# A hand-ordered recurrence on five queues: one segment of RWKV-7 and mLSTM work put into another order

## The chip, the cores and the metric

One core of one Trainium2 chip. The metric is the device time of one execution of the whole layer, in microseconds (us), taken as the median of several executions of one compiled kernel. The engines are TensorE (PE), VectorE (DVE), ScalarE (ACT), GpSimd (POOL) and the sync engine (SP), whose queue issues loads.

## What is computed

The layer has four stages in a row: a SwiGLU feed-forward, a token mixer, cross-attention over 256 memory tokens, and a second feed-forward. The change is in the token mixer, whose core is two recurrences over 1024 tokens. Cut to what matters:

```python
# RWKV-7, 8 heads of 64
state = state * w_t + (state @ -kk_t)[..., None] * (kk_t * a_t) + v_t[..., None] * k_t
y_t = state @ r_t                       # then a per-head norm, a bonus term and a gate
# mLSTM, 4 heads of 128
c = dec * c + sc * (w_end * v) @ k.T
num = p @ v + w_inter * (c_prev @ q)    # p = exp(log_d - m) * (q @ k.T)
h = num / max(|den|, exp(-m))           # then a per-head norm and a gate
```

## The kernel before, in words

The 1024 tokens are cut into eight segments of 128. One iteration of a hand-written software pipeline does the front of segment i (`front`) and the back of segment i-1 (`back`). Every engine has its own function `iteration`, and its instructions run in the order in which they are written there; between engines there are only semaphores. A list of names per engine (`F_PE`, `M_DVE` and so on) turns a name into the count that a waiting engine waits for.

The delta rule inside a segment needs the inverse of a triangular 128x128 matrix per head. It is built by doubling, in levels n = 1 to 6, with the heads in two sets, a and b. At each level TensorE forms W (from `AL` or `Ar`, and `Ur`) and V (a transpose of `Ur`) of each set, all L862; ScalarE copies them into `Wr` and `Tr`; TensorE forms E from `Tr` and `Wr`; and VectorE updates `Ur` with E (`update`, L1779 or L1783). GpSimd makes the masked matrices `AL` (L573, two for each of the levels 1 to 4). Between the two E products of a level TensorE does one step of the mLSTM (`mlstm(n)`): num at 1, dC at 3, key norms and a transpose `yT` at 4, two grams at 5 and 6. Calls of `stay_awake` are products whose result nobody reads (L786).

After level 6 come F (L774), V (L928), B (L768), and UQ (L774), which ends in `Uf` on VectorE. Then TensorE does the low-rank products `lora` of the next segment (L747, L749), Wst (L941), Z (L945) and the gate products (L949). With that the next iteration begins: Zm with Uf (L794), W1m with S0s (L797), the state products, the bonus product (L824), and transposes named kT, vT, aT, vT, bT, kT. bT (beta) writes the bank that held the bonus, so it waits for `bv` on VectorE. Then come the mean, the gram A, the variance product (L849), S, and the level 0 products A0.

On VectorE one period runs: `Uf`, two operations of the key norm (`rinv`, `kk`, by `key_root(i, 2)`), `dec` to `cc`, `gsig`, `ga`, `gu`, `kmod`, `kka` (in tile `nw`), `alpha`, `beta`, two operations on `St`, `bv`, then `Ys`, the masks of A, the variance, `U0`, `Pb`, `qe`, and the levels. The output norm of the segment before (four operations of 0.7 us, `output_norm`) stands behind level 4. GpSimd waits for its result, and finishes the output (`output`, L535 to L539), then does `bvb` (L542) and `ab` (L545) of the next iteration, and behind `kmod` four operations L547 to L553 (`rkb` twice, `kap`, `rho`).

SP loads `zs` (896 KB) for the next segment once the mask `Ab` of this one is made, then the rows `ab` and `tk`, then `zm`.

## Time and profile before

| what | us |
|---|---|
| median of 3 runs (2991.62 to 3000.18) | 2999.92 |
| profiled execution, its own time | 2997.45 |
| its span, first to last instruction | 2995.5 |
| from the start of the first segment's `Uf` to that of the eighth (seven periods) | 405.9 |

The span and the execution's own time differ by 1.95 us. The recurrence lies at about 1310 to 1827 us of the span; what is before and after it is not touched by the change. A period is counted from the start of one `Uf` to the start of the next.

### The profile page before, as it was taken

To read this page: it belongs to the slowest core of one execution; us is meant where nothing else is said; L and a number is where in the kernel's file an instruction comes from. 1 tells how busy PE (TensorE), PEld (TensorE's weight loads), DVE (VectorE), ACT (ScalarE), POOL (GpSimd) and SP (SyncE) were. 2 spreads that over 40 slices of the span, in tenths; PEclk is the share of its full clock that TensorE was granted. 3 is DMA by queue.
4 is the path that set the end of the run, shared out by engine and by line. 5 is a ranking of instruction groups with operands and counts; after the bars stand their busy time and mean duration, and the time that the engine had idled before them with its cause. 6 is when DMAs were issued, how large, how long until landed. Compare 5 with 4: busy or idle time off the path is not lost.

```text
span 2995.5 us, 38320 instructions
## 1 busy us (share of the span) xinstructions
PE 2876.2 (96%) x14927; PEld 2414.7 (81%) x14927; DVE 1281.2 (43%) x1206; ACT 579.5 (19%) x906; POOL 1219.8 (41%) x651
## 2 busy tenths in 40 slices
PE   7999999999999999969999999999999999999996
PEld 6888888888888888858888887887888888888885
DVE  5431331235556522036777765541454321431334
ACT  3100000002001121125555541110411100000011
POOL 3443333334444366624445544333044433334432
PEclk9999999999999999979989999999999999999998
DMA  3111111113222233322111203321011111111111
GB/s 133 45 46 49 49 49 49 49 44 110 99 98 98 98 110 131 118 86 45 48 33 49 51 3 131 134 77 42 0 49 44 47 49 49 49 49 49 50 40 72
DMA packets 99115, 196.61 MB, mean 66 GB/s; under 512 B 14288, under 2 KB 56400, under 8 KB 98792
## 3 DMA queue, kind: packets, MB, share of 16 engines
q1 hardware_dynamic: 80912, 139.05, 15.6%
q10 hardware_dynamic: 18136, 56.60, 5.0%
q8 instruction: 49, 0.80, 0.1%
q14 instruction: 18, 0.15, 0.0%
HBM read 160.93 MB, written 34.67 MB: 65 GB/s over the span
## 4 chain that ended last, share of the span: by engine, by line
PE 42%; issue 7%; POOL 4%; DVE 2%; ACT 1%; DMA 0%; POOLq 0%; DVEq 0%; SPq 0%; ACTq 0%
PE G L636 12%; PE G L638 12%; PE G L637 12%; PE G L1029 1%; POOL AL L573 1%; PE G L862 1%; PE G L1052 1%; POOL rkb L547 0%; PE G L849 0%; DVE xT L1986 0%; POOL ysq L558 0%; POOL rho L553 0%; POOL Ys L537 0%; PE G L1041 0%; POOL ab L545 0%
## 5 line engine op out<-in xcount | busy, mean ns | idle before, releaser
L594 POOL TENSOR_TENSOR whi<-raw,zero 128x1024 fp32r<-128x1024 f32 (+1 forms) x213 | 398.5, 1871 | 1410.3 <-PE G L638 1406.8
L636 PE MATMUL G<-hhi,whi 128*128 128x512 f32 x2288 | 893.6, 391 | 17.3 <-DVE hlo L1506 17.3
L638 PE MATMUL G<-hhi,wlo 128*128 128x512 f32 x2288 | 891.2, 390 | 0.0
L637 PE MATMUL G<-hlo,whi 128*128 128x512 f32 x2288 | 891.2, 389 | 0.0
L597 POOL TENSOR_TENSOR wlo<-raw,whi 128x1024 fp32r<-128x1024 f32 (+1 forms) x213 | 517.1, 2428 | 16.7
L636 PEld LDWEIGHTS G<-hhi,whi 128*128 128x128 f32 x2288 | 430.2, 188 | 108.8 <-issue 15.3
L638 PEld LDWEIGHTS G<-hhi,wlo 128*128 128x128 f32 x2288 | 430.1, 188 | 89.7
L637 PEld LDWEIGHTS G<-hlo,whi 128*128 128x128 f32 x2288 | 430.2, 188 | 89.3 <-issue 0.7
L636 PE MATMUL G<-ahi,whi 128*128 128x512 f32 x960 | 374.5, 390 | 2.7 <-DVEq L425 2.7
L638 PE MATMUL G<-ahi,wlo 128*128 128x512 f32 x960 | 374.2, 390 | 0.0
L637 PE MATMUL G<-alo,whi 128*128 128x512 f32 x960 | 374.2, 390 | 0.0
L636 PEld LDWEIGHTS G<-ahi,whi 128*128 128x128 f32 x960 | 180.6, 188 | 40.7 <-issue 3.1
L637 PEld LDWEIGHTS G<-alo,whi 128*128 128x128 f32 x960 | 180.5, 188 | 37.7 <-issue 0.2
L638 PEld LDWEIGHTS G<-ahi,wlo 128*128 128x128 f32 x960 | 180.6, 188 | 37.5
L1156 ACT ACTIVATE s<-s 128x1024 f32<-128x1024 f32 x44 | 46.7, 1061 | 759.7 <-DVE s L1580 759.7
L1537 DVE SCALAR_TENSOR_TENSOR xT<-G,xT 128x1024 f32 x32 | 39.2, 1225 | 292.2 <-PE G L638 292.2
L1580 DVE TENSOR_TENSOR s<-G,nrx 128x1024 f32<-128x1024 f32 x44 | 53.9, 1225 | 245.8 <-PE G L638 244.9
L1582 DVE TENSOR_TENSOR s<-s,nrx 128x1024 f32<-128x1024 f32 x44 | 132.6, 3014 | 49.6 <-ACT s L1156 49.6
L1588 DVE TENSOR_TENSOR alo<-s,ahi 128x1024 f32 x44 | 127.3, 2894 | 60.2 <-ACT ahi L1158 60.2
L1586 DVE TENSOR_TENSOR s<-s,G 128x1024 f32<-128x1024 f32 x44 | 53.8, 1222 | 224.1 <-PE G L638 223.9
L1158 ACT ACTIVATE ahi<-s 128x1024 f32 x44 | 46.7, 1062 | 418.4 <-DVE s L1586 418.4
L1597 DVE TENSOR_TENSOR po<-G,nrm 128x1024 f32<-128x1024 f32 x24 | 29.4, 1224 | 219.9 <-PE G L638 217.6
(325 smaller groups left out, 3229.7 us busy)
## 6 DMA issues: line engine op xcount, KB each, us to landing
raw<-in_wg SPq DMA_DIRECT2D x44, 512.0 KB, 3.5
raw<-in_wu SPq DMA_DIRECT2D x44, 512.0 KB, 3.5
raw<-in_wd SPq DMA_DIRECT2D x32, 512.0 KB, 3.5
raw<-in_ml_in SPq DMA_DIRECT2D x16, 512.0 KB, 3.5
zml_d<-po ACTq DMA_DIRECT2D x16, 512.0 KB, 2.6
gates_d<-po ACTq DMA_DIRECT2D x16, 512.0 KB, 2.7
zm<-zml_d SPq DMA_DIRECT2D x8, 1024.0 KB, 5.4
sg<-gates_d ACTq DMA_DIRECT2D x16, 512.0 KB, 5.0
```

The lines of the kernel that those rows point to most:

```text
L594: nc.gpsimd.tensor_tensor(hi, raw[:, k, 0:w], zero[:].to_broadcast([P, w]), ALU.add).then_inc(hi_made, 1)
L597: nc.gpsimd.tensor_tensor(lo, raw[:, k, 0:w], hi.bitcast(F32), ALU.subtract).then_inc(split_made, 1)
L636: nc.tensor.matmul(dst, wh, hi, start=start, stop=False)
L637: nc.tensor.matmul(dst, wh, lo, start=False, stop=False)
L638: return nc.tensor.matmul(dst, wl, hi, start=False, stop=stop)
L1156: activation(s0[:], s0[:], ACT.Silu).then_inc(f_silu, 1)
L1158: activation(ahi[:, i * 2 + r, :], s1[:], ACT.Copy).then_inc(a_hi, 1)
L1537: stt(x_, flat(bank_dve(c.dve + r)[:]), scale, x_, ALU.mult, ALU.add).then_inc(dve_free, 1)
L1580: tt(s0[:], flat(bank_act(c.act + r)[:]), nrx[:], ALU.mult).then_inc(act_free, 1)
L1582: tt(s0[:], s0[:], nrx[:], ALU.mult).then_inc(f_scaled, 1)
L1586: tt(s1[:], s0[:], flat(bank_dve(c.dve + r)[:]), ALU.mult).then_inc(dve_free, 1)
L1588: tt(alo[:, i * 2 + r, :], s1[:], ahi[:, i * 2 + r, :].bitcast(F32), ALU.subtract).then_inc(a_lo, 1)
```

## The change

The order of the segment's work is changed on every queue; sizes and arithmetic stay.

- VectorE: level 0 updates (`first`) ahead of the variance; `qe` right behind `bv`; the denominator and `hm` behind level 1 where they stood behind level 2; the statistics split around the second update of level 2, followed by the sum C; the four operations of the output norm set singly, at levels 3, 5, 6 and 6; `pend` ahead of the wait for A; `S0s` ahead of the wait for B and `key_root(i+1, 1)` behind it; `key_root(i, 2)` behind `kmod` of the next iteration.
- TensorE: S ahead of the variance product; W1m with S0s ahead of Zm with Uf; gate products ahead of Wst; dC at level 2, key norms at level 3; F in two halves with a wait each; the fillers ahead of A0 and at level 2 are gone in iterations with `back`, and there is one at level 4.
- ScalarE: table load and the two small activations into `lora` ahead of the copy into `Tr`; the output root behind level 1's copies; the gate's copy ahead of `Zm`'s.
- GpSimd: the masks `AL` of level 1 first, then `kw`; `ahead` (kk, ksq) behind level 2, `dec` behind level 3, `zg` last.
- SP: `zs` waits for `bv` and `vtok` in place of `Ab`.
- The last segment: three fillers at level 3 where the key norms are missing, and a small memset where the key root is.

The name lists are reordered to match and left out here; unchanged lines are cut.

```diff
...
@@ -460,7 +460,8 @@
             if front:
-                sp.wait_ge(*f_dve.at("Ab", i - 1))
+                sp.wait_ge(*f_dve.at("bv", i - 1))
+                sp.wait_ge(*f_act.at("vtok", i - 1))
...
@@ -559,10 +560,6 @@
                 return
-            pool.wait_ge(*m_act.at("D", i))
-            tt(kw[:], mktok[:], Db[:, :, SEG - 1:SEG].to_broadcast([P, MH, SEG]), ALU.mult).then_inc(*M.sig("kw"))
-            pool.wait_ge(zm_in, i * 16 + 16)
-            tt(zm[:, 12:16, :], zm[:, 12:16, :], vbc("ml_norm", SEG), ALU.mult).then_inc(*M.sig("zg"))
...
@@ -572,10 +569,17 @@
                        ALU.mult).then_inc(*F.sig(f"am{n}{x}"))
-            pool.wait_ge(*m_pe.at("num", i))
-            tt(CN[:], CN[:], Eb[:, :, SEG - 1:SEG].to_broadcast([P, MH, SEG + 1]), ALU.mult).then_inc(*M.sig("dec"))
-            if more:
-                ahead(i + 1)
+                if n == 1:
+                    pool.wait_ge(*m_act.at("D", i))
+                    tt(kw[:], mktok[:], Db[:, :, SEG - 1:SEG].to_broadcast([P, MH, SEG]), ALU.mult).then_inc(*M.sig("kw"))
+                if n == 2 and more:
+                    ahead(i + 1)
+                if n == 3:
+                    pool.wait_ge(*m_pe.at("num", i))
+                    tt(CN[:], CN[:], Eb[:, :, SEG - 1:SEG].to_broadcast([P, MH, SEG + 1]),
+                       ALU.mult).then_inc(*M.sig("dec"))
+            pool.wait_ge(zm_in, i * 16 + 16)
+            tt(zm[:, 12:16, :], zm[:, 12:16, :], vbc("ml_norm", SEG), ALU.mult).then_inc(*M.sig("zg"))
...
@@ -789,13 +793,14 @@
             if back:
+                pe.wait_ge(*f_act.at("W1c", j))
+                for n, e, r, rows in heads:
+                    nc.tensor.matmul(G[3][:, e, r * HD:(r + 1) * HD], W1m[rows, r, :], S0s[rows, r, :],
+                                     start=r == 0, stop=False, skip_group_check=True)
...
                 for n, e, r, rows in heads:
-                    nc.tensor.matmul(G[3][:, e, r * HD:(r + 1) * HD], Uf[:, n, :], Zm[:, n, :], start=r == 0, stop=False,
-                                     skip_group_check=True)
-                for n, e, r, rows in heads:
-                    last = nc.tensor.matmul(G[3][:, e, r * HD:(r + 1) * HD], W1m[rows, r, :], S0s[rows, r, :],
-                                            start=False, stop=r == RC - 1, skip_group_check=True)
+                    last = nc.tensor.matmul(G[3][:, e, r * HD:(r + 1) * HD], Uf[:, n, :], Zm[:, n, :], start=False,
+                                            stop=r == RC - 1, skip_group_check=True)
...
@@ -844,15 +849,17 @@
                 gram(alpha, beta, g1).then_inc(*F.sig("A"))
+            if front:
+                pe.wait_ge(*m_act.at("ktok", i))
+                for h in range(MH):
+                    last = nc.tensor.matmul(m0[:, h * SEG:(h + 1) * SEG], zm[:, MH + h, :], zm[:, h, :], start=True,
+                                            stop=True)
+                last.then_inc(*M.sig("S"))
...
                 return
-            pe.wait_ge(*m_act.at("ktok", i))
-            for h in range(MH):
-                last = nc.tensor.matmul(m0[:, h * SEG:(h + 1) * SEG], zm[:, MH + h, :], zm[:, h, :], start=True, stop=True)
-            last.then_inc(*M.sig("S"))
...
@@ -863,7 +870,8 @@
-            stay_awake(g2[:, 0, :], 3)
+            if not back:
+                stay_awake(g2[:, 0, :], 3)
...
@@ -872,25 +880,27 @@
                     pe.wait_ge(*m_act.at("vtok", i))
-                    pe.wait_ge(*m_dve.at("qe", i))
+                    pe.wait_ge(*m_dve.at("P", i))
...
                     last.then_inc(*M.sig("num"))
-                elif n == 3:
+                elif n == 2:
...
                     last.then_inc(*M.sig("dC"))
-                elif n == 4:
+                elif n == 3:
...
                         key_norms(i + 1)
+                    else:
+                        stay_awake(g0[:, 1, :], 3)
+                elif n == 4:
+                    stay_awake(g0[:, 1, :], 1 if back else 3)
...
                     turn(m0, hm).then_inc(*M.sig("yT"))
-                    if not back:
-                        stay_awake(g0[:, 1, :], 2)
...
@@ -900,8 +910,6 @@
                     gram(kap, rho, G[3]).then_inc(*F.sig("Mv"))
-                else:
-                    stay_awake(g0[:, 1, :], 3 if back else 4)
...
@@ -911,7 +919,7 @@
                     four(g1, e, AL[:, n % 2] if n <= MASKED else Ar, lambda n: Ur[:, n, :]).then_inc(*F.sig(f"W{n}{x}"))
-                    if n == 1:
+                    if n == 1 and e == 1:
...
@@ -921,9 +929,10 @@
                 four(g0, 1, Tr, lambda n: Wr[:, n, :]).then_inc(*F.sig(f"E{n}b"))
-            for x in SETS:
+            for e, x in enumerate(SETS):
...
-            eight(g1, Am, Ur[:].bitcast(F32)).then_inc(*F.sig("F"))
+                last = four(g1, e, Am, lambda n: Ur[:, n, :].bitcast(F32))
+            last.then_inc(*F.sig("F"))
...
@@ -936,6 +945,10 @@
                 ahead(i + 1)
+            for r in range(RC):
+                last = nc.tensor.matmul(g2[:, 0, r * P:(r + 1) * P], loraw[:, 1, r * P:(r + 1) * P], gsig[:],
+                                        start=True, stop=True)
+            last.then_inc(*F.sig("gate"))
...
@@ -945,10 +958,6 @@
             last.then_inc(*F.sig("Z"))
-            for r in range(RC):
-                last = nc.tensor.matmul(g2[:, 0, r * P:(r + 1) * P], loraw[:, 1, r * P:(r + 1) * P], gsig[:],
-                                        start=True, stop=True)
-            last.then_inc(*F.sig("gate"))
...
@@ -1245,17 +1254,20 @@
+        def lora_in(i):
+            act.wait_ge(zs_in, i * 16 + 16)
+            activation(lora[0:HD, :], zs[0:HD, 12, :], ACT.Tanh).then_inc(*l_act.sig("th"))
+            activation(lora[HD:P, :], zs[HD:P, 12, :], ACT.Copy).then_inc(*l_act.sig("ad"))
...
             tanh_exp_tables()
+            lora_in(i)
...
-            act.wait_ge(zs_in, i * 16 + 16)
-            activation(lora[0:HD, :], zs[0:HD, 12, :], ACT.Tanh).then_inc(*l_act.sig("th"))
-            activation(lora[HD:P, :], zs[HD:P, 12, :], ACT.Copy).then_inc(*l_act.sig("ad"))
...
@@ -1329,8 +1341,6 @@
                 activation(half(Ar, e), half(Am, e), ACT.Copy).then_inc(*F.sig(f"Ar{x}"))
-            if back:
-                output_root()
...
@@ -1338,6 +1348,8 @@
                 if n == 1:
+                    if back:
+                        output_root()
...
@@ -1348,19 +1360,20 @@
                     key_roots(i + 1)
+            if more:
+                tanh_exp_tables()
+                lora_in(i + 1)
...
             if more:
-                tanh_exp_tables()
...
             activation(flat(W1m[:]), g2[:, 1, :], ACT.Copy).then_inc(*F.sig("W1c"))
-            act.wait_ge(*f_pe.at("Z", i))
-            activation(flat(Zm[:]), g0[:, 0, :], ACT.Copy).then_inc(*F.sig("Zc"))
-            act.wait_ge(*f_pe.at("gate", i))
...
             activation(flat(gout[:]), g2[:, 0, :], ACT.Copy).then_inc(*F.sig("gev"))
+            act.wait_ge(*f_pe.at("Z", i))
+            activation(flat(Zm[:]), g0[:, 0, :], ACT.Copy).then_inc(*F.sig("Zc"))
...
@@ -1708,10 +1721,20 @@
-            def output_norm():
-                dve.wait_ge(*b_act.at("rsv", j))
-                newton(B, ("g1", "g2", "g3"), yrs, yve, ynw, j)
-                tt(Ys[:], Ys[:], yrs[:], ALU.mult).then_inc(*B.sig("y1"))
+            def output_norm(k):
+                r, w, v = flat(yrs[:]), flat(ynw[:]), flat(yve[:])
+                if k == 0:
+                    dve.wait_ge(*b_act.at("rsv", j))
+                    stt(w, r, -0.5, r, ALU.mult, ALU.mult).then_inc(*B.sig("g1"))
+                elif k == 1:
+                    dve.wait_ge(*B.at("g1", j))
+                    tt(w, w, v, ALU.mult).then_inc(*B.sig("g2"))
+                elif k == 2:
+                    dve.wait_ge(*B.at("g2", j))
+                    stt(r, w, 1.5, r, ALU.add, ALU.mult).then_inc(*B.sig("g3"))
+                else:
+                    dve.wait_ge(*B.at("g3", j))
+                    tt(flat(Ys[:]), flat(Ys[:]), r, ALU.mult).then_inc(*B.sig("y1"))
...
@@ -1734,6 +1757,8 @@
                     ALU.mult).then_inc(*F.sig("kmod"))
+                if back:
+                    key_root(i, 2)
...
@@ -1752,16 +1777,21 @@
                 tt(bv[:], three(g0[:, 1, :]), zs[:, 8:12, :], ALU.mult).then_inc(*F.sig("bv"))
+                dve.wait_ge(*m_act.at("E", i))
+                dve.wait_ge(zm_in, i * 16 + 16)
+                stt(flat(qe[:]), zm[:, 0:MH, :].rearrange("p h t -> p (h t)"), ML_SCALE, flat(Eb[:]), ALU.mult,
+                    ALU.mult).then_inc(*M.sig("qe"))
...
                 output_variance()
-                output_norm()
+                for k in range(4):
+                    output_norm(k)
...
-            dve.wait_ge(*f_pe.at("A", i))
...
                ALU.mult).then_inc(*F.sig("pend"))
+            dve.wait_ge(*f_pe.at("A", i))
...
@@ -1788,19 +1818,28 @@
                                           three(g1[:, e, :])).then_inc(*F.sig(f"A{x}"))
+            first(0)
+            first(1)
...
                 output_variance()
-            first(0)
-            first(1)
...
             stt(flat(Pb[:]), m0, ML_SCALE, flat(Db[:]), ALU.mult, ALU.mult).then_inc(*M.sig("P"))
-            stt(flat(qe[:]), zm[:, 0:MH, :].rearrange("p h t -> p (h t)"), ML_SCALE, flat(Eb[:]), ALU.mult,
-                ALU.mult).then_inc(*M.sig("qe"))
...
+                if n == 6 and back:
+                    output_norm(2)
...
+                if n == 2:
+                    for h in range(2):
+                        nc.vector.bn_stats(mst[:, h, :], hm[:, h, :])
+                if n == 3 and back:
+                    output_norm(0)
+                if n == 5 and back:
+                    output_norm(1)
+                if n == 6 and back:
+                    output_norm(3)
...
-                if n == 2:
+                if n == 1:
...
@@ -1810,9 +1849,14 @@
                     dve.wait_ge(*M.at("hm", i))
-                    for h in range(MH):
+                if n == 2:
+                    for h in range(2, MH):
...
                     last.then_inc(*M.sig("st"))
+                    dve.wait_ge(*m_pool.at("dec", i))
+                    dve.wait_ge(*m_pe.at("dC", i))
+                    CN4 = CN[:].rearrange("p (b h) v -> p b h v", b=2)
+                    tt(CN4, CN4, pairs_of(G[3]), ALU.add).then_inc(*M.sig("C"))
...
@@ -1821,10 +1865,6 @@
                 if n == 3:
-                    dve.wait_ge(*m_pool.at("dec", i))
-                    dve.wait_ge(*m_pe.at("dC", i))
-                    CN4 = CN[:].rearrange("p (b h) v -> p b h v", b=2)
-                    tt(CN4, CN4, pairs_of(G[3]), ALU.add).then_inc(*M.sig("C"))
...
@@ -1841,8 +1881,6 @@
                     tt(yres[:, 0:RC, bass.ds(i * SEG, SEG)], three(m0), zm[:, 12:16, :], ALU.mult).then_inc(*M.sig("y1"))
-                    if back:
-                        output_norm()
...
@@ -1851,16 +1889,16 @@
             tt(Qr[:], copies(C_ID), three(flat(g1[:])), ALU.subtract).then_inc(*F.sig("Q"))
+            dve.wait_ge(*b_dve.at("S", j))
+            tt(S0s[:], St[:], Pi[:, :, 0:1].to_broadcast([P, RC, HD]), ALU.mult).then_inc(*F.sig("S0s"))
+            dve.wait_ge(*f_pe.at("B", i))
...
                 key_root(i + 1, 1)
-            dve.wait_ge(*b_dve.at("S", j))
-            dve.wait_ge(*f_pe.at("B", i))
-            tt(S0s[:], St[:], Pi[:, :, 0:1].to_broadcast([P, RC, HD]), ALU.mult).then_inc(*F.sig("S0s"))
+            else:
+                nc.vector.memset(mnw[:], 0.0)
...
             tt(flat(Uf[:]), flat(Ur[:]).bitcast(F32), flat(g0[:]), ALU.add).then_inc(*F.sig("Uf"))
-            if more:
-                key_root(i + 1, 2)
...
```

## Rows read from the trace of the kernel before

**Rows 1.** The page: busy time by engine.

```profile
PE 2876.2 (96%) x14927; PEld 2414.7 (81%) x14927; DVE 1281.2 (43%) x1206; ACT 579.5 (19%) x906; POOL 1219.8 (41%) x651
```

**Rows 2.** Windows: seven periods, then three single ones; after POOL: clock, DMA share, GB/s.

```profile
1382.50:1788.40 405.90, 376.19 (x3428) 337.71 (x3428) 295.23 (x529) 226.80 (x464) 199.01 (x160) 0.94 0.16 37
1559.50:1620.40 60.90, 56.88 (x490) 51.11 (x490) 42.44 (x77) 32.65 (x66) 28.31 (x23) 0.89 0.15 41
1620.40:1675.70 55.30, 50.95 (x490) 45.52 (x490) 42.41 (x77) 32.84 (x68) 28.28 (x23) 1.00 0.16 45
1675.70:1734.00 58.30, 53.83 (x490) 48.25 (x490) 42.50 (x78) 32.92 (x69) 28.26 (x23) 0.94 0.23 43
```

**Rows 3.** Windows: behind the wait ahead of level 6, and low-clock stretches.

```profile
1604.50:1607.30 2.80, 1.64 (x15) 1.58 (x15) 2.71 (x6) 0.88 (x2) 1.97 (x2) 1.00 1.00 301
1607.30:1617.60 10.30, 9.79 (x52) 9.24 (x51) 4.35 (x7) 1.29 (x3) 3.88 (x4) 0.50 0.00 0
...
1723.40:1730.20 6.80, 6.29 (x37) 5.88 (x37) 2.55 (x4) 0.17 (x1) 3.05 (x3) 0.50 0.00 0
```

**Rows 4.** Timeline of TensorE: start, length, line, tile, count, [idle before, releaser].

```profile
1670.16 2.05 PE L774 MATMUL G<-Ur,Am 128*128 128x128 f32 x16 [0.51 <-DVE Ur L1783]
...
1676.13 0.37 PE L747 MATMUL G<-lora,loraw 64*128 64x128 f32 x1 [0.77 <-ACT lora L1258]
...
1677.22 1.09 PE L941 MATMUL G<-Uf,atok 128*64 128x128 f32 x16
...
1690.60 0.60 PE L762 MATMUL G<-cst,beta 128*128 128x128 f32 x4
...
1694.40 1.12 PE L849 MATMUL G<-ysq,cst 128*128 128x512 f32 x2 [0.73 <-POOL ysq L558]
...
1696.17 0.94 PE L786 MATMUL G<-idr 128*128 128x512 f32 x3
...
1698.36 0.66 PE L862 MATMUL G<-Ur,AL 128*128 128x128 f32 x4 [0.41 <-DVE Ur L1772]
...
1701.04 0.49 PE L877 MATMUL G<-mvx,Pb 128*128 128x129 f32 x2 [0.18 <-DVE qe L1798]
...
1711.32 0.66 PE L862 MATMUL G<-Ur,AL 128*128 128x128 f32 x4 [0.54 <-DVE Ur L1779]
...
1720.80 0.66 PE L862 MATMUL G<-Ur,Ar 128*128 128x128 f32 x4 [1.16 <-DVE Ur L1783]
```

**Rows 5.** Timeline of TensorE, end of the last segment, where no next segment is prepared.

```profile
1789.66 1.09 PE L941 MATMUL G<-Uf,atok 128*64 128x128 f32 x16 [1.78 <-DVE Uf L1861]
```

**Rows 6.** Timeline of VectorE in the period of rows 4.

```profile
1674.54 1.29 DVE L1705 COPY_PREDICATED Bm<-cst,G 128x1024 f32<-128x1024 uint32 x1
1675.73 1.20 DVE L1861 TENSOR_TENSOR Uf<-Ur,G 128x1024 f32<-128x1024 f32 x1
...
1683.45 0.69 DVE L1735 SCALAR_TENSOR_TENSOR kmod<-rkb,zs 128x512 f32<-128x512 f32 x1
...
1684.67 1.76 DVE L1740 TENSOR_TENSOR alpha<-kk,Pp 128x512 f32<-128x512 f32 x1
1686.35 1.52 DVE L1742 TENSOR_TENSOR beta<-nw,Pi 128x512 f32<-128x512 f32 x1
...
1689.15 0.69 DVE L1754 TENSOR_TENSOR bv<-G,zs 128x512 f32<-128x512 f32 x1
...
1693.72 0.65 DVE L1763 TENSOR_TENSOR pend<-Pp,cst 128x4 f32<-128x4 f32 x1 [0.49 <-PE G L768]
...
1699.35 1.63 DVE L1798 SCALAR_TENSOR_TENSOR qe<-zm,Eb 128x512 f32<-128x512 f32 x1
```

**Rows 7.** Timeline of GpSimd over the same period.

```profile
1668.86 1.04 POOL L542 TENSOR_TENSOR bvb<-bv,vec 128x512 f32<-128x512 f32 x1
...
1684.22 1.65 POOL L547 TENSOR_TENSOR rkb<-zs,kmod 128x512 f32<-128x512 f32 x1 [13.09 <-DVE kmod L1735]
```

**Rows 8.** Timeline of ScalarE over the same period.

```profile
1680.28 0.60 ACT L1359 ACTIVATE Zm<-G 128x512 f32<-128x512 f32 x1 [0.28 <-PE G L945]
```

More of the change, by code:

```diff
@@ L106 @@
            + [f"E{n}b"]]
-        + ["F", "V", "B", "UQ", "Wst", "Z", "gate"])
+        + ["F", "V", "B", "UQ", "gate", "Wst", "Z"])
 F_ACT = (["P", "Pi", "atok", "vtok", "btok", "ktok"] + [f"Ar{x}" for x in SETS]
-         + [f"{y}{n}{x}" for n in range(1, LEVELS) for x in SETS for y in ("Wc", "Tc")] + ["Tc", "W1c", "Zc", "gev"])
+         + [f"{y}{n}{x}" for n in range(1, LEVELS) for x in SETS for y in ("Wc", "Tc")] + ["Tc", "W1c", "gev", "Zc"])
 F_DVE = (["dec", "scan", "hend", "cc", "gs", "av", "gu", "kmod", "kka",
@@ L119 @@
 M_ACT = ["E", "nm", "ktok", "vtok", "D", "aden", "lnv", "rsv"]
-M_DVE = ["P", "qe", "dmax", "rec", "hm", "st", "mv", "ve", "C", "g1", "g2", "g3", "yn", "y1"]
-M_POOL = ["arg", "kw", "zg", "dec"]
+M_DVE = ["qe", "P", "dmax", "rec", "hm", "st", "C", "mv", "ve", "g1", "g2", "g3", "yn", "y1"]
+M_POOL = ["arg", "kw", "dec", "zg"]
 XQ_ACT = ["q"]
```

## The prediction, as put on record

> **What bounds the kernel now.** I read the page first: TensorE is busy for 96% of the span [rows 1], so nothing outside the recurrence can be won by order, and inside it only what makes TensorE wait, work for nothing, or run at a low clock. Second, the windows by period. Seven periods take 405.9 us at a mean granted clock of 0.94. A period at full clock takes 55.3; two with low stretches take 58.3 and 60.9 with the same number of products [rows 2]. At 55.3 the seven would take 387.1, so the clock costs 18.8 us. The windows inside two of them show what stands ahead of a fall: 1.64 us of busy time in 2.8, then half clock (1.2 of 2.4 GHz) for 10.3 us; elsewhere 6.8 us [rows 3]. Both begin just behind the longest wait of the period, 1.16 us at the entry of level 6, where TensorE waits for `Ur` while VectorE is in the four operations of the output norm. A period at full clock has that wait too, so the wait alone doesn't decide.
>
> Third, TensorE's timeline. I count t from the first product of Wst (L941, 1677.22). Its waits in a full-clock period are 0.77 for `lora`, 0.73 for `ysq`, 0.41 for `Ur` ahead of level 1, 0.18 for `qe`, 0.54 at level 4, 1.16 at level 6, and 0.51 ahead of F [rows 4]: 4.3 us. Three fillers ahead of A0 take 0.78 until the next product starts at 1696.95, and three more at level 2 some 0.75.
>
> Fourth, VectorE's and GpSimd's timelines side by side behind `kmod`. `kmod` takes 0.69 and, like every operation of that shape left alone, ends in time. `alpha` takes 1.76 and `beta` 1.52 for the same 128x512 elements [rows 6], and GpSimd's first `rkb` takes 1.65 where its like take 1.04 [rows 7]. The starts and ends interlock: `nw` ends at 1684.75, `rkb` at 1685.87 (1.1 later), `alpha` at 1686.43 (0.56 later), the next `rkb` at 1687.33, `beta` at 1687.87. `qe`, between two masks of GpSimd, takes 1.63, and `pend` of four columns 0.65 [rows 6]. So a VectorE operation with two operands in SBUF and a GpSimd operation run in turn, 0.55 us and about 1.05 us each; those with a PSUM operand (`bv`, `Uf`, `Bm`) don't wait.
>
> **The change part by part**, for one period at full clock, as the place where each product starts.
>
> *Around Wst.* `lora` no longer waits (0.77), and the gate products (1.02 to 0.94 us, start to start) fill the time in which `Uf` is made. From Wst to the first state product the gate is gone: -0.94. W1m's products cover the copy of `Zm`, which starts at t = 3.06 [rows 8]. The table load and both small activations lie in ScalarE's idle time behind level 6 and cost nothing; without that cover they would cost the 0.77 again. `zs` is loaded some five microseconds earlier, ahead of `ab` in the same queue, and `ab` is ready when it was.
>
> *Up to bT.* `gsig` waits for its tanh, which stands behind the copy of `Zm`: 3.06 + 0.50 + 0.33 = 3.89. `kmod` starts 1.32 later at 5.21 (before: 6.23 [rows 4, 6]) and ends at 5.9. Then `key_root(i, 2)` puts two operations with two SBUF operands here that ran beside an idle GpSimd before. Five such VectorE operations (`rinv`, `kk`, `kka`, `alpha`, `beta`) and four of GpSimd in turn: 5 x 0.55 + 4 x 1.05 = 6.95, so `beta` ends at 12.85, against 10.65 before. `St` twice and `bv` are behind it in the queue (1.97 from `beta`'s end to `bv`'s before, of which about 0.5 was waiting for products and port [rows 6]): `bv` ends near 14.3, and bT starts at 14.4. TensorE without this wait would be there at 12.44; before it was there at 13.38 [rows 4]. So the 0.94 is lost and 1.02 more: +1.96, and a new wait of 1.8 us. Queued behind bT are kT, the mean, A; all wait with it.
>
> *bT to W1.* S hides the wait of 0.73, three fillers go (0.78), `pend` leaves the path (0.57), and `U0` no longer stands behind the variance (0.6, partly beside other work): from bT to W1 6.3 us in place of 7.76 (1690.60 to 1698.36 [rows 4]): -1.46. The masks first on GpSimd are what makes the 6.3 possible: `am1a` ends near 20.1, W1 starts at 20.7.
>
> *Level 1.* num no longer waits for `qe`, and less stands between: -0.33.
>
> *Levels 2 to 4.* dC (0.87) replaces three fillers (0.75), and the wait of 0.54 goes. Put back: `aden`'s first operation comes when GpSimd has `kk` and `ksq` in hand (up to 1.05), which makes dC wait about 0.5; the norm's first operation waits for a mask (0.5) and with it W4b 0.2; `yT` waits 0.4; one filler 0.25. Sum +0.17.
>
> *Levels 5 and 6.* The norm in pieces frees `Ur` at once: -1.16 and some slack, together -1.35. F in halves starts without its 0.51: -0.69.
>
> *Up to the next Wst.* `Ys` is normalised at F - 0.3, 5 us later than now. So GpSimd's output chain (`bvb` starts 3.84 behind its first operation) reaches into VectorE's operations: `S0s` waits 0.1, and `key_root(i+1, 1)`, now ahead of `Bm`, finds `bvb` in hand and waits 1.05. `Bm` (0.34 behind `S0s` now) starts 1.2 to 1.9 later, and `Uf` with it; Wst starts 1.49 behind `Uf` [rows 4, 6]. From F to Wst: 8.5 in place of 7.06 (1670.16 to 1677.22 [rows 4]): +1.45, with TensorE idle for about 1.3 us ahead of Wst. Without the turn-taking it would be +0.6.
>
> Sum: -0.94 + 1.96 - 1.46 - 0.33 + 0.17 - 1.35 - 0.69 + 1.45 = **-1.2**, and I take -1.1, so -7.7 for seven periods. Bounds: with no turn-taking at all bT costs nothing and Wst 0.6: -4.0 a period (-28). With every pairing against VectorE once more (`rec`, `yn` behind `zg`: 1.05), 0.
>
> *Ends.* In the last segment the gate fills 0.94 of the 1.78 us ahead of Wst [rows 5]; in the first one, without fillers gone or a norm, `pend`, F and num give about 1.3, an estimate from the terms above. Together -2.3.
>
> A rule of the Trainium skill speaks against the change. The page "SBUF — State Buffer", section "Who interferes with whom", says that a VectorE operation with two SBUF inputs contends with a GpSimd one that reads SBUF, which the trace shows as above; it adds that `tensor_scalar` in its fast mode takes the same port. No row shows that here, since GpSimd is idle at `yn`. By it `yn`, four such operations now close to `zg`, could wait up to 1.05 more, and seven periods would lose 7 us of the gain.
>
> *The clock.* This is the largest unknown. The waits of 1.16 and 0.51, ahead of every fall I see, go. Two new ones come, 1.8 us ahead of bT and 1.3 ahead of Wst. One low stretch of 6.8 us costs 58.3 - 55.3 = 3.0 us [rows 2, 3]. From below: none, -18.8. From above: two in each period, 14 x 3.0 = 42.0, which is +23.2. The rows nearest are the waits of 0.73, 0.77 and 1.16: the first two no fall, the third most times. The bT wait is longer than any of them but stands among dense 512-column and transpose work, so I take one stretch in six of seven periods: 18.0, or -0.8.
>
> Total: -7.7 - 2.3 - 0.8 = -10.8, against the profiled execution's own 2997.45: **2986 us** (that execution lies 2.5 below the median shown, well inside what three runs spread).
>
> **The rivals.**
> 1. *The low clock goes.* Order gains as above and no new wait pulls the clock down: 2997.45 - 7.7 - 2.3 - 18.8 = 2969. For it: the falls all begin behind one wait, and that one is removed. Against: the new ones are as long. If in addition the turn-taking bites less, 2948 at the least.
> 2. *Slower: the clock falls twice a period.* The waits ahead of bT and of Wst each bring 6.8 us at half clock: -10.0 + 23.2 = +13, 3010. It decides as soon as more than nine stretches (28.8 / 3.0) of that length come in seven periods. For it: fillers that kept TensorE at work are gone, and 1.3 and 1.8 are above 1.16. Against: the period from 1620.4 to 1675.7, in which the wait of 1.16 brought no fall.
> 3. *It doesn't do what it says.* The waits only move, VectorE and GpSimd in turn eat all: 0 a period, 2995 to 3001.
>
> **How the numbers follow.** Forecast 0.42 (alone: 2974 to 2997), rival 1 0.24, rival 2 0.16, rival 3 0.18. The range from 2958 to 3010 leaves out about two in ten, half of it below rival 1 and half above rival 2. About 0.3% (9 us) is what a measurement of this kernel can tell from no change. Faster: two thirds of the forecast, rival 1 and a little of rival 3, 0.54. Slower: most of rival 2, 0.15. Within: 0.31.
>
> **What would show each step.** `lora`'s products start with no wait; a wait of 1 us or more stands ahead of L762 bT, released by `bv`, with `rinv`, `kk`, `alpha` and `beta` stretched to about 1.6 each. L862 behind level 5 starts with no wait. `key_root`'s L1680 takes 1.6 and a wait stands ahead of L941. GpSimd's masks start ahead of `kw`. A full-clock period reads 54 us. Wrong would be: no stretched operations (then 51 to 52), or a granted clock in the recurrence of 1.0 (rival 1) or below 0.92 (rival 2).

## The result, and the profile after

The changed kernel takes 2949.66 us (median of 4 runs, 2946.59 to 2951.97) against 2998.95 (4 runs, 2991.62 to 3000.18): ratio 0.984, interval 0.9821 to 0.9859. The prediction's sign was right, but the gain is 49 us where it gave 11, and 2949.66 lies below the range of 2958 to 3010. The profiled execution took 2946.59, its span 2944.8: 50.7 less than the span before.

The page, busy time by engine, in the form of [rows 1]:

```profile
PE 2843.2 (97%) x14892; PEld 2380.9 (81%) x14892; DVE 1292.1 (44%) x1207; ACT 579.1 (20%) x906; POOL 1227.4 (42%) x651
```

Windows of the changed kernel, with the columns of [rows 2]: the seven periods, two single ones, and a low stretch in the last segment.

```profile
1377.20:1746.10 368.90, 351.55 (x3399) 312.35 (x3400) 305.08 (x531) 226.65 (x464) 201.95 (x158) 1.00 0.19 41
1589.30:1642.10 52.80, 50.31 (x488) 44.58 (x487) 43.93 (x77) 32.87 (x68) 29.38 (x24) 1.00 0.27 47
1642.10:1694.90 52.80, 50.29 (x487) 44.54 (x486) 43.91 (x77) 32.83 (x68) 29.37 (x24) 1.00 0.22 47
1760.90:1767.70 6.80, 6.10 (x12) 4.16 (x13) 2.56 (x4) 1.26 (x2) 0.64 (x1) 0.50 0.20 62
```

In a window row the busy times stand in the order PE, PEld, DVE, ACT, POOL. The clock column reads 1.00 over all seven periods, where [rows 2] has 0.94. The seven take 368.9 in place of 405.9, so 37.0 less. Of that 18.8 is the low clock, as it was worked out ahead, and 18.2 is order: 387.1 less 368.9, about 2.5 for each period (55.3 to 52.8). The last of the seven is shorter than the others in both kernels (54.45 before, 51.14 after, each at full clock), so the split between clock and order is good to about 1 us. The rest of the 50.7 lies outside: 5.3 ahead of the first `Uf` (1382.5 to 1377.2) and 8.4 behind the last.

TensorE's timeline of one period, to be laid beside [rows 4] (start, length, line, tile, count, [idle before, releaser]):

```profile
1641.55 1.16 PE L949 MATMUL G<-gsig,loraw 128*128 128x128 f32 x8
1643.36 1.09 PE L954 MATMUL G<-Uf,atok 128*64 128x128 f32 x16 [0.66 <-DVE Uf L1901]
...
1655.12 0.60 PE L766 MATMUL G<-cst,alpha 128*128 128x128 f32 x4
1656.64 0.65 PE L766 MATMUL G<-cst,zs 128*128 128x128 f32 x4 [0.93 <-DVE St L1773]
1657.62 0.66 PE L766 MATMUL G<-cst,beta 128*128 128x128 f32 x4 [0.33 <-DVE bv L1779]
...
1663.32 0.66 PE L869 MATMUL G<-idr,AL 128*128 128x128 f32 x4 [0.30 <-DVE Am L1819]
1663.96 0.66 PE L869 MATMUL G<-Ur,AL 128*128 128x128 f32 x4
...
1684.24 0.61 PE L869 MATMUL G<-Ur,Ar 128*128 128x128 f32 x4
...
1688.21 2.00 PE L869 MATMUL G<-Ur,Am 128*128 128x128 f32 x16
...
1692.24 1.10 PE L778 MATMUL G<-Qr,Tr 128*128 128x128 f32 x8
1693.28 0.37 PE L751 MATMUL G<-lora,loraw 64*128 64x128 f32 x1
```

The waits of 1.16 ahead of level 6, 0.51 ahead of F, 0.77 ahead of `lora` and 0.73 ahead of the variance are gone. There are two large new ones: 0.66 ahead of Wst, and 0.93 + 0.33 between aT and bT. A small one of 0.30 ahead of the level 0 products stands where the three fillers stood. Read by starts, the wait between aT and bT costs more than its idle time: vT starts 1.52 behind aT and bT 0.98 behind vT, where transposes that follow without a wait start 0.44 apart (1658.12 to 1658.56), so 1.62 in all.

VectorE and then GpSimd between `kmod` and `bv`, beside [rows 6, 7]:

```profile
1648.57 0.69 DVE L1758 SCALAR_TENSOR_TENSOR kmod<-rkb,zs 128x512 f32<-128x512 f32 x1
1649.18 0.69 DVE L1696 SCALAR_TENSOR_TENSOR rinv<-nw,rinv 128x512 f32<-128x512 f32 x1
1649.90 1.65 DVE L1698 TENSOR_TENSOR kk<-kk,rinv 128x512 f32<-128x512 f32 x1
1651.58 1.42 DVE L1763 TENSOR_TENSOR nw<-kk,ga 128x512 f32<-128x512 f32 x1
1652.92 1.67 DVE L1765 TENSOR_TENSOR alpha<-kk,Pp 128x512 f32<-128x512 f32 x1
1654.51 1.67 DVE L1767 TENSOR_TENSOR beta<-nw,Pi 128x512 f32<-128x512 f32 x1
...
1656.89 0.68 DVE L1779 TENSOR_TENSOR bv<-G,zs 128x512 f32<-128x512 f32 x1
```

```profile
1649.34 1.65 POOL L548 TENSOR_TENSOR rkb<-zs,kmod 128x512 f32<-128x512 f32 x1 [7.22 <-DVE kmod L1758]
1651.08 1.37 POOL L550 TENSOR_TENSOR rkb<-rkb,vec 128x512 f32<-128x512 f32 x1
1652.41 1.63 POOL L552 TENSOR_TENSOR kap<-kmod,Pi 128x512 f32<-128x512 f32 x1
1654.00 1.63 POOL L554 TENSOR_TENSOR rho<-zs,Pp 128x512 f32<-128x512 f32 x1
```

The turn-taking is there as foretold. The operations on either engine are stretched alike and their ends interlock, and `beta` ends at 1656.18, 12.82 behind the first Wst product (foretold 12.85).

### The profile page after: what moved, and what is told of

The parts are those of the page before. It is cut to its first block, busy times and chain, and to the rows that moved or that the text cites. A ratio compares the mean times of both kernels' runs of the same rounds, so it can differ in the third digit from the quotient of the medians.

```text
span 2944.8 us, 38257 instructions
## 1 busy us (share of the span) xinstructions
PE 2843.2 (97%) x14892; PEld 2380.9 (81%) x14892; DVE 1292.1 (44%) x1207; ACT 579.1 (20%) x906; POOL 1227.4 (42%) x651
## 4 chain that ended last, share of the span: by engine, by line
PE 47%; DVE 5%; issue 2%; ACT 1%; POOL 1%; DMA 0%; DVEq 0%; SPq 0%; ACTq 0%; POOLq 0%
PE G L640 12%; PE G L642 12%; PE G L641 12%; PE G L869 4%; PE G L1038 1%; PE G L772 1%; PE G L1061 1%; PE G L958 1%; PE G L766 1%; DVE kk L1698 0%; DVE ylo L1931 0%; DVE beta L1767 0%; DVE Am L1819 0%; PE G L892 0%; PE G L954 0%
```

## The experiments

Each ran on a chip with its own runs of the kernel before, and a ratio holds inside its batch. A period and its low clock are read from each profile as above.

**a1: the output norm back in one block.** In the changed kernel all four operations stand behind level 4's `yres` again.

```diff
-                if n == 6 and back:
-                    output_norm(2)
...
                     tt(yres[:, 0:RC, bass.ds(i * SEG, SEG)], three(m0), zm[:, 12:16, :], ALU.mult).then_inc(*M.sig("y1"))
+                    if back:
+                        for k in range(4):
+                            output_norm(k)
```

> The changed kernel with the four operations of the output norm back in one block behind level 4. Theory A (the clock fell because TensorE stood still at the entry of level 6, and it no longer does): the wait there is back at about 1.3 us, a full-clock period is 53.4 to 54.0 in place of 52.8, and low-clock stretches of 6.8 us return in about half or more of the seven periods, 3 us each: 2962 to 2975. Theory B (the clock came back by the rest of the order, or by the length of the period): the wait is back, the seven periods stay at a granted clock of 1.0, and only the wait is paid: 2953 to 2958.

Measured: 2976.2 (9 runs, 2962.1 to 2984.63), ratio 0.9915 (0.9889 to 0.9941). TensorE's wait ahead of level 6, then the windows of the low stretch behind it and of the one period that had the wait but no fall:

```profile
1593.72 0.66 PE L869 MATMUL G<-Ur,Ar 128*128 128x128 f32 x4 [1.16 <-DVE Ur L1813]
```

```profile
1594.30:1604.50 10.20, 10.20 (x56) 9.86 (x55) 4.04 (x6) 4.29 (x7) 4.79 (x4) 0.50 0.09 26
1608.40:1661.60 53.20, 50.24 (x489) 44.71 (x488) 42.97 (x78) 32.78 (x67) 28.08 (x23) 1.00 0.27 47
```

The old wait comes back to the hundredth in six periods, and in five of them the clock falls within 2.1 us behind it, some 44 us at 0.50 in all. The seventh period has no such wait, but a stretch of 30.7 us at 0.50 that begins 0.2 us behind a wait of 0.60 ahead of dC (1747.63). The changed kernel has that wait too (0.59 at 1724.52) and no fall behind it, so those 30.7 us can't be put down to the norm. The profiled execution is the slowest of the nine. At full clock the edit costs only 0.4 a period, 53.2 against 52.8, since the wait of 0.66 ahead of Wst goes as the 1.16 comes (Wst starts at 1609.73 without one). So nearly all of the loss (26 us between the medians, 22 by the two ratios) is clock.

**a2: `bv` later by 1.5 us.** Three memsets of 128x512 stand ahead of it in the changed kernel.

```diff
                 dve.wait_ge(*b_pool.at("bvb", j))
+                if back:
+                    for t in (ynw, yve, yrs):
+                        nc.vector.memset(t[:], 0.0)
                 tt(bv[:]...
```

> The changed kernel with three memsets of 128x512 on VectorE ahead of bv (work added, result unchanged), so that TensorE's wait ahead of the transpose bT grows from about 1.3 us to about 2.8. If only the length of a wait decided over the clock, every period would fall to half clock behind it: 1.5 a period plus 3 a period, 2980 or more. If what decides is the wait together with the products around it, the clock stays at 1.0 in the seven periods and the time is 2950 + 7 x 1.5 = 2960.

Measured: 2971.01 (5 runs, 2967.51 to 2977.21), ratio 0.9911 (0.9884 to 0.9939). The waits in front of vT and bT, and the low stretch that begins inside the second:

```profile
1616.44 0.65 PE L766 MATMUL G<-cst,zs 128*128 128x128 f32 x4 [0.93 <-DVE St L1773]
1618.99 1.12 PE L766 MATMUL G<-cst,beta 128*128 128x128 f32 x4 [1.90 <-DVE bv L1782]
```

```profile
1618.00:1624.80 6.80, 5.81 (x27) 4.09 (x28) 2.37 (x6) 4.39 (x9) 1.04 (x1) 0.50 0.48 135
```

Every period now has a low stretch (30.6 us in seven). In six of them one begins within 1.1 us of the end of the wait ahead of bT, in the seventh 8.5 us behind it. The wait at this place does reach the clock once it is 2.8 us long; at 1.26 it doesn't. The 1.8 of the prediction lies between and was not run.

**b1: before, with only the norm in pieces.**

```diff
+                if n == 6 and back:
+                    output_norm(2)
                 update(n, 0)
+                if n == 3 and back:
+                    output_norm(0)
+                if n == 5 and back:
+                    output_norm(1)
+                if n == 6 and back:
+                    output_norm(3)
                 update(n, 1)
```

> The kernel before with this one part of the change: the four operations of the output norm set singly at levels 3, 5, 6 and 6. Theory A: the wait of 1.16 us at level 6 is gone, a full-clock period is about 54.2 in place of 55.3 (less where the output chain of GpSimd now meets VectorE at the end), and the seven periods run at a clock of 1.0: 2999 - 8 - 19 = 2972, and no less than 15 us gained. Theory B: the clock stays at 0.94, and only the wait is gained: 2991.

Measured: 3025.68 (6 runs, 3013.6 to 3030.56), ratio 1.0088 (1.0063 to 1.0114): slower. VectorE with one GpSimd row, then TensorE, ahead of Wst:

```profile
1555.01 1.47 DVE L1680 TENSOR_TENSOR nw<-nw,ssc 128x512 f32<-128x512 f32 x1
1556.40 1.49 DVE L1875 TENSOR_TENSOR S0s<-St,Pi 128x256 f32<-128x256 f32 x1
1555.89 1.72 POOL L545 TENSOR_TENSOR ab<-ab,cst 128x512 f32<-128x512 f32 x1
1557.82 1.29 DVE L1705 COPY_PREDICATED Bm<-cst,G 128x1024 f32<-128x1024 uint32 x1
1559.00 1.21 DVE L1878 TENSOR_TENSOR Uf<-Ur,G 128x1024 f32<-128x1024 f32 x1
```

```profile
1551.78 2.05 PE L774 MATMUL G<-Ur,Am 128*128 128x128 f32 x16 [0.51 <-DVE Ur L1794]
1557.74 0.37 PE L747 MATMUL G<-lora,loraw 64*128 64x128 f32 x1 [0.77 <-ACT lora L1258]
1560.26 1.97 PE L941 MATMUL G<-Uf,atok 128*64 128x128 f32 x16 [1.36 <-DVE Uf L1878]
```

The level-6 wait is gone, but GpSimd finishes the output later and now takes turns with `nw` and `S0s`. There are three waits in 9 us, the last of them 1.34 to 1.36. Six periods have it, and in four of them the clock falls at it, for 17.1 us each. Three stretches of 3.4 us begin elsewhere, 78.6 us in seven periods. A full-clock period reads 55.7.

**b2: before, with five fillers in level 5.** Nothing else moves.

```diff
                     gram(beta, rho, G[3]).then_inc(*F.sig("Mu"))
+                    if back:
+                        stay_awake(g0[:, 1, :], 5)
```

> The kernel before with five products that nobody reads (1.1 us at full clock) between the gram and the second E product of level 5, where TensorE would otherwise stand still at the entry of level 6. No engine's other order is changed. If standing still brings the clock down: clock 1.0 in the seven periods, a period of 55.3 to 55.6, 2975 to 2982. If it doesn't: 2999 to 3003 with clock 0.94. This separates the price of the clock from that of the wait.

Measured: 2981.03 (7 runs, 2979.15 to 2983.36), ratio 0.9945 (0.9928 to 0.9962). TensorE's timeline and the windows:

```profile
1537.40 1.45 PE L786 MATMUL G<-idr 128*128 128x512 f32 x5
```

```profile
1383.70:1773.70 390.00, 367.09 (x3463) 328.19 (x3463) 295.27 (x530) 226.56 (x464) 198.92 (x160) 0.99 0.18 39
1494.20:1549.50 55.30, 52.10 (x495) 46.45 (x495) 42.41 (x78) 32.84 (x67) 28.26 (x23) 1.00 0.17 45
```

The wait of 1.16 is gone, the fillers take its time (the period stays 55.3), and low clock shrinks from 47.7 to 6.8 us. This prices the clock without any change of order: 405.9 to 390.0 in the periods.

**a5: gate products behind Z again**, in the changed kernel, with their copy behind `Zm`'s.

```diff
-            for r in range(RC):
-                last = nc.tensor.matmul(g2[:, 0, ...], loraw[:, 1, ...], gsig[:], start=True, stop=True)
-            last.then_inc(*F.sig("gate"))
             pe.wait_ge(*f_dve.at("Uf", i))
```

> The changed kernel with the gate products, and their copy, back behind Z. The wait ahead of Wst grows from 0.66 to about 1.6 us. Theory A (a wait of over about a microsecond among the small products of the levels and the state brings the clock down): low-clock stretches begin behind Wst in most periods; 2970 to 2990. Theory B (only the wait at level 6 does so): order alone, 0.2 to 0.9 a period, 2951 to 2956.

Measured: 2981.05 (10 runs, 2972.77 to 2987.45), ratio 0.9926 (0.9906 to 0.9946). TensorE's timeline, and two periods in windows:

```profile
1605.19 1.93 PE L950 MATMUL G<-Uf,atok 128*64 128x128 f32 x16 [1.72 <-DVE Uf L1902]
```

```profile
1490.10:1550.10 60.00, 57.64 (x485) 52.26 (x485) 43.30 (x78) 32.87 (x68) 28.51 (x23) 0.86 0.17 42
1550.10:1603.90 53.80, 50.18 (x485) 44.50 (x485) 43.90 (x77) 32.94 (x68) 29.36 (x24) 1.00 0.22 46
```

Losing the cover costs 1.0 a period at full clock. The wait of 1.72 to 1.75 stands in six of the seven periods; in four of them the clock falls within 1.8 us behind it (58.2 us, and 3.4 more that begin elsewhere).

**a6: the stretch from A to level 1 as before** (variance ahead of S and of `U0`, `pend` behind the wait for A, three fillers, `first(0)` and `first(1)` behind the variance, and the wait for `ve` ahead of V of both sets), in the changed kernel.

```diff
+            if back:
+                pe.wait_ge(*b_pool.at("ysq", j))
+                nc.tensor.matmul(g2[:, 1, :], ...).then_inc(*B.sig("var"))
             if front:
                 pe.wait_ge(*m_act.at("ktok", i))
...
-            if back:
-                pe.wait_ge(*b_pool.at("ysq", j))
-                nc.tensor.matmul(g2[:, 1, :], ...).then_inc(*B.sig("var"))
...
-            if not back:
-                stay_awake(g2[:, 0, :], 3)
+            stay_awake(g2[:, 0, :], 3)
...
-                    if n == 1 and e == 1:
+                    if n == 1:
```

> The changed kernel with the stretch from A to level 1 as before: S behind the variance product, three fillers ahead of A0, the level 0 updates behind the variance, pend behind the wait for A. If this stretch is worth what its term said, a full-clock period is 54.2 to 54.3 in place of 52.8 (1.42 us, from the transpose bT to W1) and the time 2960 with the clock at 1.0. If the stretch only moves the wait (GpSimd's masks, made first, would have to wait for it anyway), less than 0.7 a period, 2950 to 2955. The rival on the clock: with waits of 0.73 and 0.41 back here, low-clock stretches return, 2965 or more.

Measured: 2966.47 (4 runs, 2965.99 to 2966.99), ratio 0.9882 (0.9844 to 0.9919). Windows of a full-clock period and of the only low stretch in the seven:

```profile
1486.10:1540.40 54.30, 50.65 (x490) 45.10 (x489) 44.35 (x77) 33.10 (x68) 28.96 (x24) 1.00 0.20 46
1578.90:1599.40 20.50, 20.50 (x109) 19.71 (x108) 9.94 (x18) 8.24 (x14) 5.35 (x5) 0.50 0.18 51
```

The part costs 1.5 a period (54.3 against 52.8), as its term said. One long low stretch came as well. It begins 1.5 us behind level 4's wait of 0.43, which stands in the other periods too and brings nothing there.

That wait has a likely cause of its own. The operation `mve` of four columns (a `tensor_scalar` from SBUF to SBUF) falls into the middle of a GpSimd operation here and ends with it, after 0.92 in six periods. In the changed kernel it starts 0.05 ahead of a GpSimd operation and takes 0.17. (The row of `AL` joins two operations.) The updates of `Ur` for level 4 stand behind it. a6, then the changed kernel:

```profile
1574.27 0.92 DVE L1865 TENSOR_SCALAR mve<-mmv 128x4 f32<-128x4 f32 x1
1572.64 2.52 POOL L570 TENSOR_TENSOR AL<-Am,cst 128x512 fp32r<-128x512 f32 x2
1577.44 0.66 PE L869 MATMUL G<-Ur,AL 128*128 128x128 f32 x4 [0.43 <-DVE Ur L1808]
```

```profile
1674.86 0.17 DVE L1866 TENSOR_SCALAR mve<-mmv 128x4 f32<-128x4 f32 x1
```

**b3: before, with the norm in pieces and the covers of `lora` and Wst** (gate products, table load and activations early, `S0s` ahead of the wait for B, `key_root(i+1, 1)` behind it).

```diff
+            for r in range(RC):
+                last = nc.tensor.matmul(g2[:, 0, ...], loraw[:, 1, ...], gsig[:], start=True, stop=True)
+            last.then_inc(*F.sig("gate"))
             pe.wait_ge(*f_dve.at("Uf", i))
...
+            if more:
+                tanh_exp_tables()
+                lora_in(i + 1)
             act.wait_ge(*f_pe.at("V", i))
...
+            tt(S0s[:], St[:], ...).then_inc(*F.sig("S0s"))
             dve.wait_ge(*f_pe.at("B", i))
+            if more:
+                key_root(i + 1, 1)
```

> The kernel before with the norm in pieces (which alone made it slower) and with the end of the segment as in the changed kernel: lora's inputs and table load early, gate products ahead of Wst, S0s ahead of the wait for B, key_root(i+1, 1) behind it. Theory A (the pieces need a cover for the later Uf, and these two parts together give back the clock): no wait over 0.8 us, clock 1.0 in the seven periods, full-clock period 54.0 to 54.6, 2960 to 2970, that is some three quarters of the change's gain. Theory B (masks first, S ahead of the variance, and the rest of the order are needed for it): 2985 or more.

Measured: 2988.04 (8 runs, 2981.32 to 3000.0), ratio 0.9942 (0.9913 to 0.997). A full-clock period takes 55.7, and low clock is 27.3 in seven. Theory A's 2960 to 2970 was missed: without the stretch from bT to level 1 there is no order gain, and waits of 1.12 ahead of Wst, 0.69 ahead of the product of `Zm` and `Uf`, and 0.73 ahead of the variance still stand in the period. None of the waits of 1.11 to 1.13 has a fall at it; behind the 0.69 one follows within 2.6 us in three of the seven periods.

**a3, a7 and a4: the key norm elsewhere**, in the changed kernel. a3 moves `rinv` and `kk`, a7 the two operations of `key_root(i+1, 0)` and `(i+1, 1)`, a4 both.

```diff
# a3
                 tt(dec[:], cum[:], hend[:]...).then_inc(*F.sig("cc"))
+                if back:
+                    key_root(i, 2)
...
-                if back:
-                    key_root(i, 2)
# a7
+                if n == 6 and more:
+                    key_root(i + 1, 0)
                 update(n, 1)
...
-                key_root(i + 1, 0)
+                key_root(i + 1, 1)
             dve.wait_ge(*f_pe.at("F", i))
...
-            if more:
-                key_root(i + 1, 1)
-            else:
-                nc.vector.memset(mnw[:], 0.0)
+            nc.vector.memset(mnw[:], 0.0)
```

> The changed kernel with the four operations of the key root off two paths. The last two (rinv, kk) move from behind kmod to between cc and gsig, where VectorE waits 1.40 us for the tanh and GpSimd is idle; the first goes between the output norm's last operation and the second update of level 6, the second behind Mv; a memset of four columns stays in front of Bm. Theory A (turn-taking of VectorE and GpSimd makes bv and Uf late): beta ends 3.7 us behind kmod in place of 6.9 and the waits of 0.93 and 0.33 ahead of the transposes go; Uf comes 1.2 to 1.4 us earlier and the wait of 0.66 ahead of Wst goes; a period is 50.9 to 51.3 in place of 52.8, and 2950 becomes 2935 to 2939. If the lateness came from the number of VectorE operations alone, the stretched operations would stay and at most half of it would be gained.

> The changed kernel with one part taken back: the two operations `rinv` and `kk` of the next key norm (`key_root(i, 2)`) stand between `cc` and `gsig`, where VectorE is idle for 1.40 us and GpSimd has no work of this kind, in place of behind `kmod`. Theory A (these two operations, run in turn with GpSimd's four, are what bT waits for): the 0.93 ahead of vT and the 0.33 ahead of bT go, a full-clock period takes 51.5 in place of 52.8, and seven periods give -8.8: 2941, plus up to 3 if one or two short low stretches come. The wait of 0.66 ahead of Wst stays. Rival B (bT's wait comes from the queue behind beta, `St` and `bv`, whatever stands ahead of it): the period stays above 52.4 and the time above 2946.

> The changed kernel with only the other half of the key norm moved: `key_root(i+1, 0)` behind level 6's first half, `key_root(i+1, 1)` behind the mask of Mv, a memset of four columns where it stood ahead of Bm; `rinv` and `kk` stay behind `kmod`. Theory A (the 1.51 us operation between `S0s` and `Bm` is what Wst waits for): the wait of 0.66 ahead of Wst goes, waits ahead of vT and bT stay at 0.93 and 0.33, a full-clock period takes 52.1 to 52.2, the time is 2945. Rival B (the two halves only help together, or the time freed ahead of Wst comes back as a longer wait ahead of vT): 2949 or more.

| kernel | median us (runs) | ratio (interval) | full-clock period | low clock in seven |
|---|---|---|---|---|
| a4 | 2935.47 (5) | 0.9765 (0.9733 to 0.9796) | 50.7 | 6.8 |
| a3 | 2936.53 (4) | 0.9796 (0.9778 to 0.9814) | 51.2 | 0 |
| a7 | 2946.3 (4) | 0.9828 (0.981 to 0.9846) | 52.3 | 0 |

a3's VectorE: `rinv` and `kk` in time, `nw` too, and only `alpha` and `beta` in turn, as in [rows 6].

```profile
1587.22 0.68 DVE L1696 SCALAR_TENSOR_TENSOR rinv<-nw,rinv 128x512 f32<-128x512 f32 x1
1587.94 0.69 DVE L1698 TENSOR_TENSOR kk<-kk,rinv 128x512 f32<-128x512 f32 x1
...
1590.64 0.69 DVE L1763 TENSOR_TENSOR nw<-kk,ga 128x512 f32<-128x512 f32 x1
1591.24 1.76 DVE L1765 TENSOR_TENSOR alpha<-kk,Pp 128x512 f32<-128x512 f32 x1
1592.92 1.53 DVE L1767 TENSOR_TENSOR beta<-nw,Pi 128x512 f32<-128x512 f32 x1
```

The period falls by 1.6, just the 1.62 read from the starts of vT and bT: theory A, and rival B is out. It is more than the two operations' own length: from the start of `kmod` to the end of `beta` it is 4.42 in place of 7.61, 3.2 less, where `rinv` and `kk` take 1.4 alone. a7 takes 0.5 where 0.66 was expected: a wait of 0.31 for `Qr` appears ahead of UQ. Together they give 2.1, a4's 50.7. By their intervals a4 and a3 beat the changed kernel (0.984, 0.9821 to 0.9859); a7's overlaps it, and for a7 only the period tells. a4 and a3 end level in their medians (their ratios come from two batches, whose kernels before took 3008.33 and 2997.26), in the profile too (357.6 for the seven periods of each), where a4 has two short low stretches and a3 none.

## Why the prediction was wrong

**The step that failed is the clock.** The prediction put it so: "The bT wait is longer than any of them but stands among dense 512-column and transpose work, so I take one stretch in six of seven periods: 18.0, or -0.8." There was none in any period: -18.8, which is rival 1. Of the 39.9 us between the 10.8 foretold and the 50.7 of the profile, this term is 18.0, the ends are 11.4 and the order of the periods is 10.5. (It also took every stretch as 6.8 us; the five of the kernel before average 9.5.) The half of its reasoning that was right is that the falls of the seven periods stand behind the wait of 1.16. Putting it back brings falls behind it in five periods of six (a1), and filling it in the kernel before leaves 6.8 us of low clock where there were 47.7 (b2). What was wrong was to take the new waits as equally harmful. They came out smaller: 0.66 in place of 1.3 ahead of Wst, and in place of 1.8 ahead of bT one of 0.93 and one of 0.33 with four transposes between them. Larger waits at the same two places do bring the falls back: 0.93 and 1.90 ahead of bT (a2), 1.72 ahead of Wst (a5), and in b1 1.36 ahead of Wst, about what was foretold. So the size of the new waits is the likely reason; that the falls would have come with just the waits foretold was not run for bT.

**The order gain was right in its signs, but for levels 2 to 4, and mis-sized in three parts.** By starts in a full-clock period: Wst to the state products -0.75 (foretold -0.94), to bT +1.63 (+1.96), bT to W1 -1.42 (-1.46), level 1 -0.38 (-0.33), levels 2 to 4 -0.46 (+0.17), level 5 -1.32 (-1.35), level 6 -0.72 (-0.69), F to Wst +0.91 (+1.45). The sum is -2.5 where -1.2 was worked out and -1.1 taken: 18.2 us for seven periods in place of 7.7. The difference is 1.3. Three put-backs were charged too high, by 0.63, 0.54 and 0.33, and the first term too good by 0.19. Up to bT these nearly cancel: +0.88 together against +1.02. The list of small waits in levels 2 to 4 (0.5, 0.2 and 0.4) came to one of about 0.3 by starts ahead of dC (0.14 of idle time). From F on, `S0s` isn't stretched (0.41) and `key_root`'s L1693 takes 1.51, so `Bm` starts 5.52 behind F where it was 4.38: 1.14 later, below the 1.2 to 1.9 foretold. Wst then starts 1.26 behind `Uf`, not 1.49, and the wait ahead of it is 0.66, not 1.3.

**The ends gave 13.7, not 2.3.** In the last segment the wait of 1.78 [rows 5] is now 0.45 (0.84 was foretold), and a low stretch of 13.7 us that began 2 us behind it went too. The windows of before:

```profile
1791.60:1805.30 13.70, 13.70 (x100) 12.80 (x101) 5.49 (x4) 5.57 (x7) 4.41 (x2) 0.50 0.26 87
```

From the last `Uf` to the mean product it is 19.2 before (1788.40 to 1807.59) and 12.1 after (1746.07 to 1758.15): 7.1 of the 8.4. A new stretch of 6.8 us (1760.90 to 1767.70, shown above) begins behind it. The prediction counted the low clock only inside the seven periods. Ahead of the first `Uf` 5.3 were gained against 1.3; a low stretch of 3.4 us near 1350 us is gone there too, worth 1.2 to 1.5 at the prices listed at the end. Waits of 0.98 and 0.16 ahead of level 1, of 0.81 at a later level and of 0.60 ahead of F went with it, 2.55 of idle time.

**Point by point.** Right: `lora` without a wait; a new wait at the transposes with `kk` to `beta` stretched to 1.4 to 1.7 (`rinv`, before GpSimd had started, was not); no wait behind levels 5 and 6; L1693 at 1.51 and a wait ahead of Wst; granted clock 1.0, named as rival 1's sign. Wrong: a full-clock period of 54 (52.8), and a wait of 1 us or more ahead of bT released by `bv`; ahead of bT stand 0.33, and the 0.93 stands ahead of vT, released by `St`. The page "SBUF — State Buffer" of the Trainium skill, section "Who interferes with whom", was cited for two things. On the two-input case the trace agrees (1.65 and 1.65 side by side, 0.69 alone, and a3's 1.6 a period). Its `tensor_scalar` clause cost nothing at `yn`, which never ran beside GpSimd. But a6 agrees with it: `mve` took 0.92 beside GpSimd against 0.17. The prediction's "No row shows that here" holds for `yn` alone: in the first segment of the kernel before `mve` (L1822) already takes 1.06.

The sum now reads: clock 18.8, order 18.2, head 5.3, tail 8.4, together 50.7. Over the whole span the low clock goes from some 132 us to 68; at the 18.8 for 47.7 of the periods that is an estimated 25 us, about half of the gain. By b2 the first is worth 15.9 without any order; b1, b3 and a5 show that the parts don't add: the norm in pieces alone loses 0.9%, and keeps its gain only with something for TensorE to do while `Uf` is made.

**Open.** What brings the clock down isn't settled. The same wait in the same place doesn't always do it, counted in the seven periods: 1.16 ahead of level 6 in five periods of six (before, and again a1), 1.72 to 1.75 ahead of Wst in four of six (a5), 1.34 to 1.36 there in four of six (b1). One of 1.11 to 1.13 ahead of Wst never did directly (b3), though it is nearly as long as the 1.16. One of 1.26 spread over two transposes never did (changed kernel, a7). a4 fell behind 0.30 and a6 for 20.5 us behind 0.43. No wait's length alone sorts these. The place within the period may matter, but was not isolated.

## What to carry to other kernels

Where the engine that bounds shows a granted clock under 1.00, price the clock over the whole stretch, ends included, and ask of each wait removed and each wait made how long it becomes: here about half of the gain was order. Try fillers in the longest wait first; it is one line, and it separates the clock from the order. Operations of VectorE with two SBUF operands belong where GpSimd is idle: moving two of them ahead of `gsig` took 1.6 off a period of 52.8, and the ratio from 0.984 to 0.980, each in its own batch.

## What was unexpected of the hardware

- A wait of 1.16 us in a period that is busy for 92% (53.83 of 58.30, [rows 2]) is followed by 6.8 to 17.1 us at 1.2 GHz, and one of 1.36 behind two shorter ones by 17.1 us (b1). The low clock costs less than half of its length: 18.8 for 47.7 us in the periods before, 3.0 for 6.8 in one of them, 8.5 for 20.5 in a6 (62.8 against 54.3), 4.6 for 13.7 in a5 (58.5 against 53.8).
- Five products whose result nobody reads, 1.45 us, gave back 15.9 us in seven periods.
- A low stretch can come behind idle time of only 0.30 (a4, 1451.4 to 1454.8 us of its span, 2.75 behind the wait).
- A VectorE operation of four columns can take 0.92 in place of 0.17 when it starts in the middle of a GpSimd operation (a6).
